# Six spare weight chunks instead of four in a mixture-of-experts loop, with GpSimd copying two of them

## The reference, cut to what matters

```python
logits = xt @ w_router + b_router                 # 512 x 32
top_val, top_idx = lax.top_k(logits, 4); gates = softmax(top_val)
def expert_block(args):                           # one expert e and one block of its tokens
    e, x_b = args
    gu = x_b @ w_gu[e] + b_gu[e]                  # 1024 x 2048
    gate = minimum(gu[..., ::2], 7); up = clip(gu[..., 1::2], -7, 7)
    return ((up + 1) * (gate * sigmoid(1.702 * gate))) @ w_dn[e] + b_dn[e]   # 1024 x 1024
y[t] = sum over the four experts of t of gates * yb;  x = x + mx[5] * rms_norm(y, g_post_ffn)
```

## Time and profile before

| what | us |
|---|---|
| median of three runs (lowest to highest) | 2890.73 (2877.65 to 2892.95) |
| the profiled execution: its own time | 2882.36 |
| its span, first to last instruction | 2880.6 |
| PE busy, share of the span | 2493.6, 87% |
| DVE busy, share | 1253.4, 44% |
| expert loop, first to last matmul | 1167.3 to 2222.2 |

### The profile page before, as it was taken

How to read it: one execution, slowest core, us unless ns; L and a number is a source line. 1 busy time by engine, 2 the same in 40 slices (tenths; PEclk the granted TensorE clock), 3 DMA queues, 4 the chain that set the end, 5 groups by cost and what they waited for, 6 DMA issues and landing times. The chain is left out here.

```text
span 2880.6 us, 62057 instructions
## 1 busy us (share of the span) xinstructions
PE 2493.6 (87%) x23388; PEld 1218.8 (42%) x23388; DVE 1253.4 (44%) x2324; ACT 694.8 (24%) x1558; POOL 453.0 (16%) x384
## 2 busy tenths in 40 slices
PE   5888888856889996799999998999898699789998
PEld 3456565645564443233333332333233254455444
DVE  2263747463257426344444444544454512643012
ACT  3133333343061013111111111121111411354000
POOL 0031213130070000211111111111110101154000
PEclk8998989878899997899999999999999699989999
DMA  6000000000308325799999999599987421001221
GB/s 256 27 28 25 6 25 6 4 2 32 111 8 332 135 73 209 272 423 424 424 424 424 423 424 423 221 424 423 423 339 286 157 88 69 20 3 66 73 73 58
DMA packets 114812, 552.07 MB, mean 192 GB/s; under 512 B 13633, under 2 KB 17217, under 8 KB 63202
## 3 DMA queue, kind: packets, MB, share of 16 engines
q1 hardware_dynamic: 97234, 510.79, 43.9%
q0 software_dynamic: 6912, 20.98, 1.9%
q10 hardware_dynamic: 10512, 18.08, 1.8%
HBM read 734.74 MB, written 16.52 MB: 261 GB/s over the span
## 5 line engine op out<-in xcount | busy, mean ns | idle before, releaser
L1517 PE MATMUL moe_gu_ps<-expert_w,xgT 128*32 128x512 f32 x6016 | 683.2, 601 | 62.0 <-PEq L1450 61.9
L1517 PEld LDWEIGHTS moe_gu_ps<-expert_w,xgT 128*32 128x32 f32 x6016 | 231.2, 111 | 496.7 <-issue 496.7
L1537 PE MATMUL moe_down_ps<-expert_w,actT 128*32 128x512 f32 x3008 | 346.3, 593 | 14.0 <-PEq L1450 14.0
L1438 ACT ACTIVATE xgT<-xt,ffn_shift,ffn_gain 128x64 f32<-128x64 f32 x384 | 137.6, 429 | 785.5 <-ACTq L1450 785.5
L1624 DVE COPY expert_w<-b_w 128x2048 f32 x188 | 231.7, 1233 | 171.6 <-DVEq L1450 158.7
L1537 PEld LDWEIGHTS moe_down_ps<-expert_w,actT 128*32 128x32 f32 x3008 | 114.2, 110 | 228.2 <-issue 227.3
L1631 DVE TENSOR_TENSOR biased<-moe_gu_ps,b_gu 128x1024 f32<-128x1024 f32 x47 | 57.6, 1225 | 250.1 <-DVEq L1450 250.1
L1429 POOL DMA_INDIRECT xg<-normed_rows,tokens x96 | 150.7, 1570 | 82.9 <-POOLq L1450 68.3
L1499 POOL COPY tokens<-token_of 128x2 uint32 x47 | 8.6, 182 | 816.0 <-POOLq L1450 816.0
L521 PE MATMUL b2p_ps<-b_w,b_hT 128*128 128x512 f32 (+1 forms) x320 | 121.3, 542 | 2.9 <-PEq L66 2.9
L521 PE MATMUL b2g_ps<-b_w,b_hT 128*128 128x512 f32 x256 | 111.7, 599 | 0.7 <-PEq L57 0.7
(11 more groups left out here) (593 smaller groups left out, 3587.1 us busy)
## 6 DMA issues: line engine op xcount, KB each, us to landing
expert_w<-in_w_experts SPq DMA_DIRECT2D x384, 1024.0 KB, 9.9
b_w<-in_w_experts SPq DMA_DIRECT2D x192, 1024.0 KB
late_w<-in_w_late SPq DMA_DIRECT2D x12, 2048.0 KB, 9.1
b_w<-in_w_in SPq DMA_DIRECT2D x10, 2048.0 KB, 7.5
begin_w<-in_w_ada SPq DMA_DIRECT2D x6, 2048.0 KB, 17.6
slot_rows<-yb ACTq DMA_DIRECT2D x94, 128.0 KB
mix_w<-in_w_in_tok SPq DMA_DIRECT2D x4, 2048.0 KB, 11.2
x<-in_w_rkv SPq DMA_DIRECT2D x4, 1536.0 KB, 6.5
```

Source lines behind the costliest of these rows:

```text
L1438: made = nc.scalar.activation(xgT[:, k, :, :], xt[:, :, k, :], ACT.Identity, scale=gain[:, k:k + 1], bias=shift[:, k:k + 1])
L1517: made = nc.tensor.matmul(ps_gu[UNIT * j:UNIT * j + UNIT, u, :], xgT[:, k, u, :], w[:, k, 512 * j:512 * j + 512], start=(k == 0), stop=(k ...
L1537: made = nc.tensor.matmul(ps_dn[to:to + UNIT, :], actT[:, u, c, :], w[:, i, at:at + 512], start=(c == 0), stop=(c == KD - 1), skip_group_c ...
```

## The change

It raises the spares to six. DVE still copies chunks 0 to 3; POOL copies chunks 4 and 5, after its gather. The spares lie partly in the second block's `hT`. Expert 1 is put second in the table by a fixed key, so that its first chunks can be loaded before the table is known: four while routing goes on, two at the start of the loop. The stage `moe_end` is folded into the loop's stage. In `finish_ffn` PE adds two of the four expert rows with diagonal share matrices that ACT makes, and DVE the other two.

```diff
+                for k in range(2):
+                    weights.load_second(sp, k)
                 sp.wait_ge(s["expert"], 2)
                 sp.dma_start(table[0:1, :], experti[:, 0:1]).then_inc(s["table"], 16)
+                sp.wait_ge(s["rows"], 16)
+                for k in (3, 4):
+                    weights.load_second(sp, k)
                 sp.wait_ge(s["table"], 16)
-                sp.wait_ge(s["rows"], 16)
...
                 step(nc.vector.memset(key[:, 0:1], -1.0))
+                step(nc.vector.memset(key[:, 1:2], -0.5))
...
-SPARES = 4
+SPARES, BY_POOL = 6, 2
...
+    def load_second(self, sp, k):
+        sp.dma_start(self.spare[k], self.source[1, k]).then_inc(self.spare_here[k], 16)
...
+                for k in (2, SPARES - 1):
+                    weights.load_second(sp, k)
                 here, after, later = (expert_at(slice(j, j + 1)) for j in range(3))
                 for k in range(SPARES):
-                    load_spare(k, after, here)
-                for k in range(SPARES):
-                    takes(sp, s["spare_free"])
+                    takes(sp, s["spare_free" if k < SPARES - BY_POOL else "back_free"])
                     load_spare(k, later, after)
                 for i in range(SPARES, GU):
                     load(i, after, here)
...
                     for k in range(SPARES):
-                        takes(sp, s["spare_free"])
+                        takes(sp, s["spare_free" if k < SPARES - BY_POOL else "back_free"])
                         load_spare(k, later, after)
...
                     gather_block(s["xg_here"])
+                    for k in range(SPARES - BY_POOL, SPARES):
+                        takes(pool, s["back_used"])
+                        takes(pool, spare_here[k], 16)
+                        nc.gpsimd.tensor_copy(w[:, bass.ds(DUMP + 1 - (DUMP + 1 - k) * (after != here), 1), :],
+                                              spare[k].unsqueeze(1)).then_inc(s["moved"], 1)
+                        takes(pool, s["moved"])
+                        nc.gpsimd.sem_inc(s["back_here"], 1)
+                        nc.gpsimd.sem_inc(s["back_free"], 1)
...
-                            takes(pe, s["front_here"])
+                            takes(pe, s["front_here" if k < SPARES - BY_POOL else "back_here"])
...
-                    for k in range(SPARES):
+                    for k in range(SPARES - BY_POOL):
                         takes(dve, s["front_used"])
...
+BY_VECTOR = 2
...
+                pe.wait_ge(arrived[m], 16 * TOP_K)
+                for j in range(BY_VECTOR, TOP_K):
+                    for c in range(2):
+                        last = nc.tensor.matmul(ps_b[:, m % banks, 512 * c:512 * c + 512],
+                                                share_diag[:, m, j - BY_VECTOR, :],
+                                                taken[:, m * TOP_K + j, 512 * c:512 * c + 512], start=False,
+                                                stop=(j == TOP_K - 1), skip_group_check=True)
                 last.then_inc(s["biases"], 1)
...
+            for m in range(NT_X):
+                for j in range(BY_VECTOR, TOP_K):
+                    last = nc.scalar.activation(share_diag[:, m, j - BY_VECTOR, :], g.ident[:, :], ACT.Copy,
+                                                scale=weight[:, m, j:j + 1])
+                last.then_inc(s["share_diag"], 1)
...
-                for j in range(TOP_K):
+                for j in range(BY_VECTOR):
                     rows, share = taken[:, m * TOP_K + j, :], weight[:, m, j:j + 1]
```

More of the change, by code:

```diff
@@ L878, in ffn_block @@
                         early=first_loads, first=make_affine, n_first=2)
-        route_stage(nc, tables, g, hT_next, ones, y, rows, weight, slot_of, of_expert, token_of, table, n_blocks,
-                    *ring.slots)
+        route_stage(nc, tables, weights, g, hT_next, ones, y, rows, weight, slot_of, of_expert, token_of, table, n_blocks,
+                    ring.slots[0])
         routing.close()
-        slot_rows = experts(nc, d, g, weights, ring, rows, gain, shift, token_of, table, n_blocks)
+        slot_rows = experts(nc, d, g, weights, rows, gain, shift, token_of, table, n_blocks)
         moving.close()
@@ L1130, in load, with route_stage @@
             sp.dma_start(to, source).then_inc(self.loaded, 16)
[L1133 to L1134 removed]
+def route_stage(nc, tables, weights, g, hT, ones, xn, rows, weight, slot_of, of_expert, token_of, table, n_blocks,
+                spare):
     with ExitStack() as held:
@@ L1382, in __init__ @@
         self.source = d["w_experts"]
+        halves = [ring.slots[i][:, 4 * j:4 * j + 4, :].rearrange("p k n -> p (k n)") for i in (1, 0) for j in (0, 1)]
+        self.spare = [halves[0], halves[1], hT[:, 4:8, :].rearrange("p k n -> p (k n)"), halves[2], halves[3],
+                      hT[:, 0:4, :].rearrange("p k n -> p (k n)")]
+        self.spare_here = [held.enter_context(nc.semaphore(f"spare{k}_here")) for k in range(SPARES)]
     def load_first(self, sp):
@@ L1386, in load_first, with experts @@
             sp.dma_start(self.w[:, i], self.source[0, i]).then_inc(self.arrived[i], 16)
-def experts(nc, d, g, weights, ring, rows, gain, shift, token_of, table, n_blocks):
+    def load_second(self, sp, k):
+        sp.dma_start(self.spare[k], self.source[1, k]).then_inc(self.spare_here[k], 16)
+def experts(nc, d, g, weights, rows, gain, shift, token_of, table, n_blocks):
     ident = g.ident[:, :]
@@ L1399, in experts @@
     GU, DUMP = KD, CHUNKS
-    spare = [ring.slots[k // 2][:, 4 * (k % 2):4 * (k % 2) + 4, :].rearrange("p k n -> p (k n)") for k in range(SPARES)]
+    spare, spare_here = weights.spare, weights.spare_here
     with ExitStack() as held:
@@ L1483, in _ @@
                         load(i, here, before)
+                for here in [*spare_here, *arrived[SPARES:GU]]:
+                    sp.wait_ge(here, 16)
             @block.gpsimd
@@ L1493, in gather_block, with expert_at @@
                     nc.gpsimd.sem_inc(here, 1)
+                def expert_at(place):
+                    return pool.value_load(table[0:1, place], min_val=0, max_val=N_EXP - 1)
                 takes(pool, s["first_tokens"])
@@ L1701, in _, with biases @@
             last.then_inc(s["turned"], 1)
+            def biases(m):
+                for c in range(2):
+                    nc.tensor.matmul(ps_b[:, m % banks, 512 * c:512 * c + 512], of_expertT[:, m, :],
+                                     b_dn[:, 512 * c:512 * c + 512], start=True, stop=False, skip_group_check=True)
+            pe.wait_ge(s["kept"], 1)
+            pe.wait_ge(s["loaded"], 16)
+            biases(0)
             for i in range(2):
@@ L1708, in _ @@
                 last.then_inc(s["rows"], 1)
-            pe.wait_ge(s["kept"], 1)
-            pe.wait_ge(s["loaded"], 16)
+            pe.wait_ge(s["share_diag"], NT_X)
             for m in range(NT_X):
                 if m >= banks:
-                    pe.wait_ge(s["summed"], (m - banks) * TOP_K + 1)
-                for c in range(2):
-                    last = nc.tensor.matmul(ps_b[:, m % banks, 512 * c:512 * c + 512], of_expertT[:, m, :],
-                                            b_dn[:, 512 * c:512 * c + 512], start=True, stop=True)
+                    pe.wait_ge(s["summed"], (m - banks) * BY_VECTOR + 1)
+                if m:
+                    biases(m)
+                pe.wait_ge(arrived[m], 16 * TOP_K)
+                for j in range(BY_VECTOR, TOP_K):
+                    for c in range(2):
+                        last = nc.tensor.matmul(ps_b[:, m % banks, 512 * c:512 * c + 512],
+                                                share_diag[:, m, j - BY_VECTOR, :],
+                                                taken[:, m * TOP_K + j, 512 * c:512 * c + 512], start=False,
+                                                stop=(j == TOP_K - 1), skip_group_check=True)
                 last.then_inc(s["biases"], 1)
```

36 lines of the change are left out of this document (15 added, 21 removed).

## The result

| | before | after |
|---|---|---|
| median of four runs (lowest to highest), us | 2890.45 (2877.65 to 2892.95) | 2915.15 (2912.69 to 2923.21) |
| the profiled execution, and its span | 2882.36, 2880.6 | 2912.69, 2910.9 |

A forecast was written before the change was run, and what follows sets the result against it. It took the expert loop to live near two limits, DMA at 424 GB/s and PE. 4.5 + 3 + 4 + 0.5 - 2.5 - 0.5 + 1 = +10 on 2890.7 gave 2900 us, range 2883 to 2921.

The forecast's parts named there:

- the port rival: Expert loop: DVE and POOL copies block one another in 17 turns, 24 us instead of 4; +30, say 2915; chance 0.28.
- Part 3: POOL's copies and gather in the expert loop: rows come later, DVE's copies slip by 3.2 us; +4, bounds 0 and 24.
- it just fits: DVE's slipped copies end at 16.7 us, 17.5 with 0.8 added, where the bias addition is due at 17.7.
- part 2: Second DMA-full stretch, turns 29 to 34: SP waits for POOL's copy, 4 us of DMA idle; +3, bounds 0 and 8.
- Part 1: First DMA-full stretch: two more spares go ahead of urgent chunks in a full queue; +4.5 us, bounds 0 and 4.9.
- It isn't won back: The first stretch's +4.5 us stays lost, since turns 28 to 30 are bound by PE.
- The last turn: Chunks 10 and 11 wait for `back_free` at 18.9 us against their use at 18.9 and 20.6; +0.5, bounds 0 and 3.
- Folding `moe_end`: After the last store: of 2.8 us, mostly the store's landing, folding saves 0.5; bounds 0 and -2.8.
- Part 4: The edges: the end stage, with eight of DVE's 16 row sums gone, is 2.5 us shorter; bounds +1 and -10.3.
- ACT is late next: End stage: ACT's eight turned columns come ahead of its square and can start only 2.5 us earlier.
- Routing and the first gather: Ahead of the loop: the table, for which SP waits, queues behind two more chunks; +1 us, bounds 0 and 4.9.

The follow-up runs named there:

- e1: The changed kernel, with POOL issuing the next gather ahead of its two copies and awaiting its landing after them: 2898.03 us, 1.0044 against the kernel before.
- e5: The changed kernel with POOL copying only 128 of 2048 columns of chunks 4 and 5, the rest left out: 2901.92 us, 1.0040 against the kernel before.
- e9: The kernel of e1 with each of POOL's two copies made twice: 2907.03 us, 1.0077 against the kernel before.
- e10: The kernel of e1 again, unchanged: 2892.97 us, 1.0020 against the kernel before.
- e6: The changed kernel with three spares, all copied by DVE, chunk 3 loaded ahead of 8 and 9: 2889.61 us, 1.0012 against the kernel before.
- e3: The changed kernel with four spares, all copied by DVE: 2884.01 us, 0.9990 against the kernel before.
- e7: The changed kernel with five spares, one copied by POOL, the next gather issued ahead of that copy: 2885.02 us, 1.0003 against the kernel before.
- e11: The kernel of e3 again, unchanged: 2886.52 us, 1.0000 against the kernel before.
- e4: The kernel before with only the new end stage, PE adding two of four expert rows: 2887.54 us, 1.0006 against the kernel before.
- e8: The kernel before once more, unchanged, one execution: 2893.69 us.

## Why the prediction was right and wrong

**The result, 2915, is the port rival's and not the forecast's 2900.** By the medians the change costs 24.7, by the ratio some 31; by the traces, without the part that no changed line touches, 20.4; the forecast was 10. The rival's mechanism is what the runs show. That its number came out too is partly luck: its blocking was put at 24 us, and about 11 can be read in the trace.

**Part 3 is the step that failed**, where it says that DVE's copies end at 16.7, "it just fits". Its pieces held: POOL's copy is 1.89 (2.0 taken), and the rows reach DVE 9.4 after a bias addition (2194.36 to 2203.76) where they took 7.5; over the nine turns without a chunk wait it is 9.4 to 11.9, so 1.9 to 4.4 late for the 3.2 forecast. But it let DVE's last two copies slip into the time of POOL's and went on pricing them at 1.23, and left the blocking to a rival, with a chance of 0.28. The first makes the second: copies that slip fall under POOL's, take 2.0 to 2.5, hold POOL's second copy, and so the next gather. In the turn shown PE starts at 2196.18 and DVE's fourth copy ends at 2214.83, 18.65 into it: the forecast had 16.7, the rival 19.2. With two tenths of slack that is enough for a turn of 21.2. The nine turns of the last stretch that take 20.6 before, without a chunk wait (T29 to T33, T41 to T46), take 21.2 to 23.2, 10.6 us together, 1.2 each; the rival's 1.4 was near. What it had wrong was the number, 17: the others lie in the stretch bound by bytes, where a late turn seems to be mostly won back from the loads that ran on (T5 to T29 costs 1.7). The rest of T29 to T46 is +2.2, from T33 to T41, and that is part 2's. e1 takes the term away, and e5 and e9 bear on its two halves.

That one copy waits for the other's whole can be read off: DVE's copy of 2191.59 was issued 0.95 before POOL's end at 2192.54, and 0.95 + 1.23 = 2.18 against 2.02 in the trace; POOL's of 2190.45 was issued 0.34 before DVE's end (2188.37 + 2.42), and 0.34 + 1.89 = 2.23 against 2.09. Sharing at half speed would give, by an estimate, 1.23 + 0.95 / 2 = 1.7 for the first. The Trainium skill ("SBUF — State Buffer", SBUF: two separate sides) tells of such an exclusive lock for the whole instruction, and here the trace agrees to 0.16 us.

**Part 1 held**: +4.1 from T1 to T5 (+4.5), its size following the number of spares. T0 to T5 shows only 2.4, since T0 to T1 ran 1.7 shorter than before; that interval lies between 19.5 and 22.1 over the runs. Against four spares with the same T0 to T1 it is 3.3 to 3.9. "It isn't won back" held for six spares; for five it didn't, and why five come out ahead wasn't taken apart.

**Part 2 held in mechanism** (3.4 idle us in turn 31 for 4). What it costs is read best in e1, where T33 to T34 takes 25.0 for 20.9, as forecast, and the turns to T41 give most of it back: +1.2 and, in e10, +1.6 for the +3.

**The last turn** had its 0.5 from chunks 10 and 11. These aren't what PE waits for: the gate is late with the bias addition. 2.45 of the 3.0 us came with the lower granted clock, which e5 and e6 show without the longer idle time too; no step had the clock in it. Folding `moe_end`, put at -0.5, isn't to be seen: with the full clock the last turn takes 18.5 to 18.7 with the fold (e1, e3, e7, e11) and 18.0 to 18.2 without it (before, e4, e8).

**Part 4** forecast -2.5 and got -0.6 (-1.0 alone in e4), both inside the scatter of that stage. "ACT is late next" is right to the row. PE's work was mis-sized, though not its matmuls: I took the four of the source at 0.86, 3.5 a tile, and the trace has eight of 0.46, 3.70. Left out was the next tile's bias product between them, which makes it 5.54 a tile. So PE sets the pace and the turned columns come late.

**Routing and the first gather**: +0.6 for +1, the sum of +2.5 in routing and -1.9 in a first gather that meets a shorter queue. Neither was in the forecast by itself.

**Open.** How much of the last turn's clock is the change's. Why six spares with the gather first lose between 2.9 and 6.7 by T29 in two executions. No version here beats the kernel before: four spares (1.0000, 0.9990) and five with the gather first (1.0003) are level with before. By its trace the five-spare loop is 2.4 us shorter from T1 to T46, a tenth of a per cent, which its ten runs can't show.

## What to carry to other kernels

Before giving POOL work that DVE has no time for, lay both engines' copies of a turn on one time axis, with the slip that the change itself causes: a wait that grows with the collision it makes can become the new turn. Then ask of each stretch whether its wait really ends last, since any way round a loop adds up to the turn. Start what others wait for (the gather) ahead of the long copies on the same engine, and let the copies end before the next chain on the other engine begins; two long copies of DVE and POOL at once gained nothing here. In a DMA queue that is full, depth for one buffer is delay for another, so try the number of spares in both directions.

## What the runs showed that was not expected

- PE idle for 2.36 us in the last turn was followed by a granted clock of 1.00 in before and seven other runs, and by 0.57 and 0.61 over the next 4 us in e5 and e6; idle for 4.20 was followed by 0.50. The same wait can cost 1.6 us or nothing.
- The first gather took 4.7 to 4.8 us from issue to use with one weight chunk in the queue, 8.7 with four: worth 4 us ahead of T0 (T0 is 4.4 to 4.8 earlier, counted from that gather's issue, in e3, e11 and e6).
- A gather's two issues take 1.51 and 1.72 beside DVE's copies (e1) and 0.97 and 0.95 in the kernel after, where they come before them: the late place makes the issues cheaper (990 ns mean for 1587 in e1), and it was still the slower kernel.
- A copy of 128 columns on POOL takes 0.29 us alone, one of 2048 takes 1.89: a sixteenth of the columns costs more than a seventh of the time.
- The bias addition on DVE, which reads the matmuls' result, takes 1.22 to 1.23 us beside a POOL copy as well, where DVE's copies and the gate's first operation are held.
